# A two-layer decoder trunk on one core: the first transfers cut smaller and spread over both queues, the first x tile's upper part made on VectorE, ten warm-up products for fifteen

## Chip, core and metric

The kernel runs on one core of a Trainium2 chip. The metric is the time of one execution on the device in microseconds (us). The kernel before takes 419.99 us, the median of three runs from 419.8 to 420.08.

## What is computed

Two layers over x, 256 tokens of 1024 numbers in float32. Each layer normalises its input, projects it, mixes along the tokens, gates with SiLU and projects back. Layer 0, with whose first projection the kernel starts, is this:

```python
def rms_norm(x, g):
    xf = x.astype(jnp.float32)
    y = xf * lax.rsqrt(jnp.mean(xf * xf, axis=-1, keepdims=True) + EPS)
    return (y * g.astype(jnp.float32)).astype(x.dtype)

def pool_layer(x, norm_g, w_in, w_pool, pool_scale, w_out):
    h = rms_norm(x, norm_g)
    u, z = jnp.split(h @ w_in, 2, axis=-1)          # 1024 -> 2048 + 2048
    y = pool_mixer(u, w_pool, pool_scale) * jax.nn.silu(z)   # moving sums of 2, 4, 8, 16 tokens
    return x + y @ w_out                            # 2048 -> 1024
```

Layer 1 has the same frame with w_in 1024 -> 4 x 2048 (q, k, v, z) and causal attention in 16 heads of 128 as its mixer; with 256 tokens there is one block, and no block choice takes part.

## The kernel before

The order of the work is written out by hand: one program for each engine, tied by semaphores. SyncE (SP) and ScalarE (ACT) each issue transfers on a queue of their own; both queues are served by the same 16 DMA engines.

Every product of two float32 matrices is made as three products in fp32r: each operand is split into an upper part (rounded to fp32r, names ending in _hi) and a lower part (what is left, _lo), and hi x hi, hi x lo and lo x hi are added up. ScalarE makes the upper parts by copying (`w_hi`, line 413 for the first pieces; `hT_hi`, line 410, which also multiplies by the norm's gain), VectorE the lower parts by subtracting (`w_lo`, line 866; `hT_lo`, line 876).

The weights come in granules of 1 MB (four 128x512 blocks) into a ring of four buffers, `raw`. The first two granules belong to the first 512 columns of w_in0 and are loaded block by block, eight transfers of 256 KB on SP's queue (line 245), so that work can start on the first block. Meanwhile ScalarE's queue brings the norm's gains (16 KB, line 375) and x transposed, `xT` (part of the buffer `wide`; eight tiles of 128x256), as four transfers of 256 KB, two tiles in each (line 377).

The useful work starts in `early_granule`: eight stages, one for each x tile. In a stage TensorE multiplies one weight block by one x tile: four products hi x hi, four with `w_lo`, four with `hT_lo` (line 656). For stage i ScalarE makes `hT_hi` of tile i, then `w_hi` of block i; VectorE then makes `w_lo` of block i and `hT_lo` of tile i. TensorE waits for `h0_hi` and `piece_hi` ahead of a stage, for `piece_split` ahead of its second four products and for `h0_split` ahead of its third.

Until the data are there, TensorE runs 15 warm-up products of zeros (line 697), float32, 128x128, each of which is two passes in the trace. ScalarE's first instruction is a dummy exponential (line 379) that has the function table loaded early; in its program it stands behind the transfers that ScalarE issues.

Of the kernel before, what the change touches and what calls it, by code (L numbers as in the profile page):

```python
# [9 lines left out]
ALU = mybir.AluOpType  # L10
ACT = mybir.ActivationFunctionType
# [14 lines left out]
KD = D_MODEL // P  # L26
KI = D_INNER // P
COLS = 512
GK = 4
GROUPS = D_INNER // COLS  # L30
HPG = COLS // HEAD_DIM
RING = 4
EDGE = max(POOL_WINDOWS)
PADDED = EDGE + SEQ
WARM_UP = 15
MASKED = -1e30
NO_MAX = -3.4e38

# [15 lines left out]
def constant_tables():  # L54

    edge = np.stack([w / np.minimum(np.arange(EDGE) + 1, w) for w in POOL_WINDOWS]).astype(np.float32)
    edge = np.ascontiguousarray(np.broadcast_to(edge.reshape(1, -1), (P, GROUPS * EDGE)))
    inv = np.float32(ROPE_THETA) ** (-np.arange(0, HEAD_DIM, 2, dtype=np.float32) / np.float32(HEAD_DIM))
# [30 lines left out]
def bass_hybrid_trunk(nc, x, w_in0, w_pool0, w_out0, w_in1, w_out1, xT_in, gains_in, qk_gains, table, edge_table,  # L89
                      out):  # L90
    with ExitStack() as ctx:
        def sb(name, shape, dt=F32):
            return ctx.enter_context(nc.sbuf_tensor(name, shape, dt))

        def sem(name):
            return ctx.enter_context(nc.semaphore(name))


        raw = sb("raw", [P, RING, GK * COLS])
        w_hi = sb("w_hi", [P, RING, GK * COLS], F32R)  # L100
        w_lo = sb("w_lo", [P, RING, GK * COLS], F32R)
        xs = sb("xs", [P, TT, D_MODEL])
        hT_hi = sb("hT_hi", [P, KD, SEQ], F32R)
# [4 lines left out]
        uT = sb("uT", [P, HPG, PADDED])  # L108
        edges = sb("edges", [P, GROUPS, EDGE])
        rstd_b = sb("rstd_b", [P, SEQ])  # L110
# [10 lines left out]
        gains = sb("gains", [P, 2 * KD + KI])  # L121
# [28 lines left out]
        xT = wide[:, :, :].rearrange("p t n -> p (t n)")[:, 2 * D_MODEL:].rearrange("p (k s) -> p k s", k=KD)  # L150
# [19 lines left out]
        zeros_made = sem("zeros_made")  # L170
        raw_landed = [sem(f"raw_landed{i}") for i in range(RING)]
        ident_made, gains_landed = sem("ident_made"), sem("gains_landed")
        edges_landed, table_landed = sem("edges_landed"), sem("table_landed")
        diag_made, rstd_spread, rstd_b_made = sem("diag_made"), sem("rstd_spread"), sem("rstd_b_made")
        pooled_made = sem("pooled_made")
        x_landed, xT_landed = sem("x_landed"), [sem(f"xT_landed{b}") for b in range(KD // 2)]
        piece_landed = [[sem(f"piece_landed{n}{k}") for k in range(GK - 1)] for n in range(2)]
        piece_hi, piece_split = sem("piece_hi"), sem("piece_split")
        h0_hi, h0_split = sem("h0_hi"), sem("h0_split")
        half_hi = [sem("half_hi0"), sem("half_hi1")]  # L180
        half_split = sem("half_split")
        hi_made = sem("hi_made")
# [42 lines left out]
        w_in0_v = w_in0.rearrange("(k p) n -> p k n", p=P)  # L225
# [6 lines left out]
        def _(sp):  # L232
            def load(slot, src, n=None):
                if n is not None:
                    sp.wait_ge(w_split, n - RING + 1)
                sp.dma_start(raw[:, slot, :].rearrange("p (k n) -> p k n", k=GK), src).then_inc(raw_landed[slot], 16)
# [3 lines left out]
                load(j, src, n)  # L240


            for i in range(2 * GK):
                n, k = i // GK, i % GK
                sp.dma_start(raw[:, n, k * COLS:(k + 1) * COLS],
                             w_in0_v[:, i, 0:COLS]).then_inc((*piece_landed[n], raw_landed[n])[k], 16)
# [42 lines left out]
            for i in range(8 * GROUPS + 8):  # L289
# [8 lines left out]
                if i < 8 * GROUPS:  # L298
                    g, j = divmod(i, 8)
                    src = w_in1_v[:, (j % 2) * GK:(j % 2 + 1) * GK, bass.ds((j // 2) * D_INNER + g * COLS, COLS)]  # L300
                    load(j % RING, src, N_L1 + 8 * g + j)
                else:
# [70 lines left out]
        @block.scalar  # L373
        def _(act):
            act.dma_start(gains[:, :], gains_in).then_inc(gains_landed, 16)
            for b in range(KD // 2):
                act.dma_start(xT[:, 2 * b:2 * b + 2, :], xT_in[:, 2 * b:2 * b + 2, :]).then_inc(xT_landed[b], 16)
            act.wait_ge(pool_chain, 2)
            act.activation(row_sum[:, 0, 0:1], minus_half[:, 0:1], ACT.Exp)

# [24 lines left out]
            act.wait_ge(gains_landed, 16)  # L405
            for i in range(KD):
                n, k = i // GK, i % GK
                if i % 2 == 0:
                    act.wait_ge(xT_landed[i // 2], 16)
                act.activation(hT_hi[:, i, :], xT[:, i, :], ACT.Copy, scale=gains[:, i:i + 1]).then_inc(h0_hi, 1)  # L410
                act.wait_ge((*piece_landed[n], raw_landed[n])[k], 16)
                piece = slice(k * COLS, (k + 1) * COLS)
                act.activation(w_hi[:, n, piece], raw[:, n, piece], ACT.Copy).then_inc(piece_hi, 1)
            act.wait_ge(raw_landed[2], 16)
            act.activation(w_hi[:, 2, 2 * COLS:], raw[:, 2, 2 * COLS:], ACT.Copy).then_inc(half_hi[1], 1)
            for b in range(KD // 2):
                act.activation(sqT[:, 2 * b * SEQ:2 * (b + 1) * SEQ],
                               xT[:, 2 * b:2 * b + 2, :].rearrange("p k s -> p (k s)"),
                               ACT.Square).then_inc(sqT_made, 1)
# [188 lines left out]
        def _(pe):  # L608
# [32 lines left out]
            def u_tile(f):  # L641
                return acc[0][f // 2][:, (f % 2) * SEQ:(f % 2 + 1) * SEQ]

            def early_granule(n):

                for k, i, f in [(k, i, f) for k in range(GK) for i in range(3) for f in range(HPG)]:
                    if f == 0 and i == 0:
                        pe.wait_ge(h0_hi, GK * n + k + 1)
                        pe.wait_ge(piece_hi, GK * n + k + 1)
                    if f == 0 and i == 1:  # L650
                        pe.wait_ge(*((piece_split, (GK - 1) * n + k + 1) if k < GK - 1 else (w_split, n + 1)))
                    if f == 0 and i == 2:
                        pe.wait_ge(h0_split, GK * n + k + 1)
                    src, w = (hT_lo if i == 2 else hT_hi), (w_lo if i == 1 else w_hi)
                    c = k * COLS + f * P
                    ins = pe.matmul(u_tile(f), w[:, n, c:c + P], src[:, GK * n + k, :],  # L656
                                    start=(n, i, k, f % 2) == (0, 0, 0, 0), stop=(n, i, k) == (1, 2, GK - 1),
                                    skip_group_check=True)
                    if n == 1 and i == 2 and k == GK - 1 and f == 1:
                        ins.then_inc(tile0_ready, 1)  # L660
                ins.then_inc(w_used, 1)
# [33 lines left out]
            pe.wait_ge(zeros_made, 1)  # L695
            for _ in range(WARM_UP):
                pe.matmul(acc[1][1][:, 0:P], zeros, zeros, start=True, stop=True)  # L697

            early_granule(0)
            early_granule(1)  # L700

            def sum_tokens():
# [138 lines left out]
        def _(dve):  # L841
# [22 lines left out]
            def part_lo(n, a, b, made):  # L864
                part = slice(a * COLS, b * COLS)
                return dve.tensor_tensor(w_lo[:, n, part], raw[:, n, part], w_hi[:, n, part].bitcast(F32),
                                         ALU.subtract).then_inc(made, 1)

            def piece_lo(n, k):
                dve.wait_ge(piece_hi, GK * n + k + 1)  # L870
                part_lo(n, k, k + 1, piece_split if k < GK - 1 else w_split)

            for i in range(KD):
                piece_lo(i // GK, i % GK)
                dve.wait_ge(h0_hi, i + 1)
                dve.scalar_tensor_tensor(hT_lo[:, i, :], xT[:, i, :], gains[:, i:i + 1],
                                         hT_hi[:, i, :].bitcast(F32), ALU.mult, ALU.subtract).then_inc(h0_split, 1)
            dve.wait_ge(half_hi[0], 1)
# [11 lines left out]
            ins.then_inc(sqT_summed, 1)  # L890
            dve.memset(uT[:, :, 0:EDGE], 0.0)

            def u_out(g):
                for t in range(TT):
                    product_ready(dve, t, 2 * g, 4 * g + 1)
                    if t == 0:
                        dve.wait_ge(*((pooled_made, g) if g else (rstd_b_made, 1)))
                    dve.tensor_tensor(uT[:, 2 * t:2 * t + 2, EDGE:], acc[0][t][:, :].rearrange("p (f s) -> p f s", f=2),
                                      rstd_b[:, :].unsqueeze(1).to_broadcast([P, 2, SEQ]), ALU.mult).then_inc(u_made, 1)
# [58 lines left out]
            for g in range(GROUPS):  # L958
                n = N_POOL + 3 + g
# [152 lines left out]
            for j in range(6):  # L1112
# [6 lines left out]
                n = N_OUT1 + 3 + j  # L1119
# [39 lines left out]
```

## Time and profile before

| what | value |
|---|---|
| median of 3 runs | 419.99 us |
| the profiled execution | 419.89 us |
| its span, first to last instruction | 417.9 us |
| TensorE busy | 413.7 us, 99% of the span |
| VectorE, ScalarE, GpSimd busy | 292.2, 236.9, 32.0 us |
| TensorE's warm-up, line 697 | 1.04 to 7.57 us |

The span leaves out some 2 us around the program. All times within it count from its first instruction. A matmul's row in the trace overlaps with the next one's, since products are pipelined; the distance from start to start is what one costs.

### The profile page before, as it was taken

To read this page: it belongs to the slowest core of one execution; us is meant where nothing else is said; L and a number is where in the kernel's file an instruction comes from. 1 tells how busy PE (TensorE), PEld (TensorE's weight loads), DVE (VectorE), ACT (ScalarE), POOL (GpSimd) and SP (SyncE) were. 2 spreads that over 40 slices of the span, in tenths; PEclk is the share of its full clock that TensorE was granted. 3 is DMA by queue.
4 is the path that set the end of the run, shared out by engine and by line. 5 is a ranking of instruction groups with operands and counts; after the bars stand their busy time and mean duration, and the time that the engine had idled before them with its cause. 6 is when DMAs were issued, how large, how long until landed. Compare 5 with 4: busy or idle time off the path is not lost.

```text
span 417.9 us, 5551 instructions
## 1 busy us (share of the span) xinstructions
PE 413.7 (99%) x2126; PEld 354.6 (85%) x2126; DVE 292.2 (70%) x373; ACT 236.9 (57%) x430; POOL 32.0 (8%) x45
## 2 busy tenths in 40 slices
PE   9999999999999999999999999999999999999996
PEld 9989898988888888888888888888888888888885
DVE  3879987779885554428943799637996479966522
ACT  5845453525464353477837796377863978636310
POOL 0166000000000000111001010010000110000000
PEclk9999999999999999999999999999999999999999
DMA  7996769464554756337876627878478856767002
GB/s 268 385 351 217 262 199 341 152 209 169 210 177 132 207 190 201 102 100 252 300 233 221 192 103 262 254 228 273 129 263 262 249 206 183 226 245 252 0 2 100
DMA packets 45945, 86.78 MB, mean 208 GB/s; under 512 B 2528, under 2 KB 8288, under 8 KB 45920
## 3 DMA queue, kind: packets, MB, share of 16 engines
q1 hardware_dynamic: 45200, 85.37, 61.7%
q10 hardware_dynamic: 720, 1.07, 0.8%
q8 instruction: 17, 0.28, 0.3%
q14 instruction: 8, 0.07, 0.0%
HBM read 79.61 MB, written 6.82 MB: 207 GB/s over the span
## 4 chain that ended last, share of the span: by engine, by line
PE 99%; DVE 0%; issue 0%
PE acc L633 26%; PE acc L635 26%; PE acc L634 26%; PE acc L678 3%; PE acc L677 3%; PE acc L656 3%; PE acc L675 3%; PE aux L772 2%; PE acc L697 2%; PE aux L688 1%; PE aux L779 1%; PE aux L790 1%; PE aux L791 1%; PE aux L789 1%; PE aux L771 1%; DVE ysb L1129 0%
## 5 line engine op out<-in xcount | busy, mean ns | idle before, releaser
L848 DVE TENSOR_TENSOR w_lo<-raw,w_hi 128x2048 fp32r<-128x2048 f32 x65 | 147.9, 2285 | 45.2 <-ACT w_hi L384 45.2
L384 ACT ACTIVATE w_hi<-raw 128x2048 fp32r<-128x2048 f32 x64 | 122.0, 1914 | 43.9 <-PE acc L635 31.0
L633 PE MATMUL acc<-w_hi,hT_hi 128*128 128x512 f32 x320 | 127.0, 397 | 0.0
L635 PE MATMUL acc<-w_hi,hT_lo 128*128 128x512 f32 x320 | 124.8, 390 | 0.0
L634 PE MATMUL acc<-w_lo,hT_hi 128*128 128x512 f32 x320 | 124.6, 389 | 0.0
L635 PEld LDWEIGHTS acc<-w_hi,hT_lo 128*128 128x128 f32 x320 | 60.1, 188 | 12.8
L634 PEld LDWEIGHTS acc<-w_lo,hT_hi 128*128 128x128 f32 x320 | 60.2, 188 | 11.9
L633 PEld LDWEIGHTS acc<-w_hi,hT_hi 128*128 128x128 f32 x320 | 60.1, 188 | 11.8
L633 PE MATMUL acc<-w_hi,aT_hi 128*128 128x512 f32 x160 | 63.6, 397 | 0.0
L635 PE MATMUL acc<-w_hi,aT_lo 128*128 128x512 f32 x160 | 62.4, 390 | 0.0
L634 PE MATMUL acc<-w_lo,aT_hi 128*128 128x512 f32 x160 | 62.3, 389 | 0.0
L635 PEld LDWEIGHTS acc<-w_hi,aT_lo 128*128 128x128 f32 x160 | 30.0, 188 | 6.4
L634 PEld LDWEIGHTS acc<-w_lo,aT_hi 128*128 128x128 f32 x160 | 30.1, 188 | 5.9
L633 PEld LDWEIGHTS acc<-w_hi,aT_hi 128*128 128x128 f32 x160 | 30.1, 188 | 5.8
L1004 DVE CUSTOM_DVE_ANT_0 aux<-aux,mask 128x128 f32<-128x128 f32 x16 | 4.7, 296 | 37.1 <-PE aux L772 37.1
L677 PE MATMUL acc<-hT_hi,w_hi 128*128 128x256 f32 x96 | 27.2, 283 | 0.0
L678 PE MATMUL acc<-hT_lo,w_hi 128*128 128x256 f32 x96 | 27.2, 283 | 0.0
L675 PE MATMUL acc<-hT_hi,w_lo 128*128 128x256 f32 x96 | 27.2, 283 | 0.0
L483 ACT ACTIVATE probs<-aux,exp_bias,q_rstd 128x128 f32<-128x128 f32 x16 | 7.2, 451 | 26.7 <-DVE exp_bias L1008 26.6
L675 PEld LDWEIGHTS acc<-hT_hi,w_lo 128*128 128x128 f32 x96 | 18.4, 192 | 0.1
L677 PEld LDWEIGHTS acc<-hT_hi,w_hi 128*128 128x128 f32 x96 | 18.4, 192 | 0.1
L678 PEld LDWEIGHTS acc<-hT_lo,w_hi 128*128 128x128 f32 x96 | 18.4, 192 | 0.0
(126 smaller groups left out, 452.4 us busy)
## 6 DMA issues: line engine op xcount, KB each, us to landing
raw<-in_w_in_dram SPq DMA_DIRECT2D x46, 1024.0 KB, 7.0
raw<-in_w_out_dram SPq DMA_DIRECT2D x16, 1024.0 KB, 5.4
raw<-in_w_pool_dram SPq DMA_DIRECT2D x4, 1024.0 KB, 5.6
between<-wide SPq DMA_DIRECT2D x8, 512.0 KB, 3.9
raw<-in_w_in_dram SPq DMA_DIRECT2D x8, 256.0 KB, 8.0
wide<-between SPq DMA_DIRECT2D x16, 128.0 KB, 2.8
qkT<-between SPq DMA_DIRECT2D x16, 128.0 KB, 3.0
between<-uT SPq DMA_DIRECT2D x3, 512.0 KB, 10.1
```

The costliest lines, as they stand in the source:

```text
L384: act.activation(w_hi[:, slot, :], raw[:, slot, :], ACT.Copy).then_inc(hi_made, 1)
L483: act.activation(probs[:, 0:P], aux[h % 2][:, 0:P], ACT.Exp, bias=exp_bias[:, h, 0:1], scale=q_rstd[:, g % 2, 0, h:h + 1], accum_out=row_s ...
L633: pe.matmul(a, shi, whi, start=first and k == 0, stop=False)
L634: pe.matmul(a, shi, wlo, start=False, stop=False)
L635: ins = pe.matmul(a, slo, whi, start=False, stop=last and k == GK - 1)
L656: ins = pe.matmul(u_tile(f), w[:, n, c:c + P], src[:, GK * n + k, :], start=(n, i, k, f % 2) == (0, 0, 0, 0), stop=(n, i, k) == (1, 2, GK ...
L675: pe.matmul(u_tile(f), wlo, shi, start=j == 0 and k == 0 and f % 2 == 0, stop=False, skip_group_check=True)
L677: pe.matmul(u_tile(f), whi, shi, start=False, stop=False, skip_group_check=True)
L678: ins = pe.matmul(u_tile(f), whi, slo, start=False, stop=end, skip_group_check=True)
L697: pe.matmul(acc[1][1][:, 0:P], zeros, zeros, start=True, stop=True)
L772: pe.matmul(s[:, P:3 * P], qT[:, h, P:SEQ], kT[:, :, h], start=True, stop=True).then_inc(scores_ready, 1)
L848: dve.tensor_tensor(w_lo[:, slot, :], raw[:, slot, :], w_hi[:, slot, :].bitcast(F32), ALU.subtract).then_inc(w_split, 1)
```

## The change

Five edits, all at the start of the program.

- The first weight block (256 KB) is cut in two halves of 256 columns. SP issues the first half as before at the head of its queue, ScalarE issues the second half.
- ScalarE issues x in five pieces instead of four: tile 0, tile 1, then the pairs 2 and 3, 4 and 5, 6 and 7. The half weight block goes out right behind tile 0.
- VectorE makes `hT_hi` of tile 0 with its own semaphore `first_h0_hi`; ScalarE's loop starts with the first weight block and goes on with tile 1.
- TensorE waits for `first_h0_hi` in the first stage, and the counts of `h0_hi` are one lower in the others.
- Ten warm-up products instead of fifteen.

```diff
+X_PIECES = [(0, 1), (1, 2), (2, 4), (4, 6), (6, 8)]
-WARM_UP = 15
+WARM_UP = 10
...
-            for i in range(2 * GK):
+            sp.dma_start(raw[:, 0, 0:COLS // 2], w_in0_v[:, 0, 0:COLS // 2]).then_inc(piece_landed[0][0], 16)
+            for i in range(1, 2 * GK):
                 n, k = i // GK, i % GK
                 sp.dma_start(raw[:, n, k * COLS:(k + 1) * COLS],
                              w_in0_v[:, i, 0:COLS]).then_inc((*piece_landed[n], raw_landed[n])[k], 16)
...
-            for b in range(KD // 2):
-                act.dma_start(xT[:, 2 * b:2 * b + 2, :], xT_in[:, 2 * b:2 * b + 2, :]).then_inc(xT_landed[b], 16)
+            for b, (k0, k1) in enumerate(X_PIECES):
+                act.dma_start(xT[:, k0:k1, :], xT_in[:, k0:k1, :]).then_inc(xT_landed[b], 16)
+                if b == 0:
+                    act.dma_start(raw[:, 0, COLS // 2:COLS], w_in0_v[:, 0, COLS // 2:COLS]).then_inc(piece_landed[0][0], 16)
...
-                if i % 2 == 0:
-                    act.wait_ge(xT_landed[i // 2], 16)
-                act.activation(hT_hi[:, i, :], xT[:, i, :], ACT.Copy, scale=gains[:, i:i + 1]).then_inc(h0_hi, 1)
-                act.wait_ge((*piece_landed[n], raw_landed[n])[k], 16)
+                if i > 0:
+                    for b, (k0, _) in enumerate(X_PIECES):
+                        if k0 == i:
+                            act.wait_ge(xT_landed[b], 16)
+                    act.activation(hT_hi[:, i, :], xT[:, i, :], ACT.Copy, scale=gains[:, i:i + 1]).then_inc(h0_hi, 1)
+                act.wait_ge((*piece_landed[n], raw_landed[n])[k], 16 if i > 0 else 32)
...
-                        pe.wait_ge(h0_hi, GK * n + k + 1)
+                        pe.wait_ge(*((h0_hi, GK * n + k) if n or k else (first_h0_hi, 1)))
                         pe.wait_ge(piece_hi, GK * n + k + 1)
...
+            dve.wait_ge(gains_landed, 16)
+            dve.wait_ge(xT_landed[0], 16)
+            dve.tensor_scalar(hT_hi[:, 0, :], xT[:, 0, :], gains[:, 0:1], 1.0, ALU.mult, ALU.mult).then_inc(first_h0_hi, 1)
             for i in range(KD):
                 piece_lo(i // GK, i % GK)
-                dve.wait_ge(h0_hi, i + 1)
+                dve.wait_ge(*((h0_hi, i) if i else (first_h0_hi, 1)))
```

ScalarE's program from its start, before the change; `gains`, `wide` (x transposed) and `raw` (weights) are filled by its and SP's transfers, and what it waits for stands in brackets:

```order
L375 DMA gains<-in_gains_dram 128x32
L377 DMA wide<-in_xT_dram 128x512 x4
L379 ACT_TABLE_LOAD
L379 ACTIVATE row_sum<-minus_half 128x1 [waits pool_chain]
L410 ACTIVATE hT_hi<-wide,gains 128x256 [waits xT_landed0,gains_landed]
L413 ACTIVATE w_hi<-raw 128x512 [waits piece_landed00]
L410 ACTIVATE hT_hi<-wide,gains 128x256
L413 ACTIVATE w_hi<-raw 128x512 [waits piece_landed01]
```

The same stretch after the change:

```order
L377 DMA gains<-in_gains_dram 128x32
L379 DMA wide<-in_xT_dram 128x256
L381 DMA raw<-in_w_in_dram 128x256
L379 DMA wide<-in_xT_dram 128x256
L379 DMA wide<-in_xT_dram 128x512 x3
L383 ACT_TABLE_LOAD
L383 ACTIVATE row_sum<-minus_half 128x1 [waits pool_chain]
L419 ACTIVATE w_hi<-raw 128x512 [waits piece_landed00,gains_landed]
L416 ACTIVATE hT_hi<-wide,gains 128x256 [waits xT_landed1]
L419 ACTIVATE w_hi<-raw 128x512 [waits piece_landed01]
L416 ACTIVATE hT_hi<-wide,gains 128x256 [waits xT_landed2]
```

Seven transfers instead of five stand ahead of the table load, and the first `w_hi` is ScalarE's first piece of real work. VectorE's program after the change, from its first instruction:

```order
L850 MEMSET k_s 128x128
L882 TENSOR_SCALAR hT_hi<-wide,gains 128x256
L873 TENSOR_TENSOR w_lo<-raw,w_hi 128x512
L886 SCALAR_TENSOR_TENSOR hT_lo<-wide,gains,hT_hi 128x256
L873 TENSOR_TENSOR w_lo<-raw,w_hi 128x512
```

Its second row is new; before, the first `w_lo` (line 866) stood right behind the memset, and all that follows is as it was.

## Rows read from the trace of the kernel before

**Rows 1.** The page: span, TensorE's busy time, granted clock in 40 slices.
```profile
span 417.9 us, 5551 instructions
PE 413.7 (99%) x2126; PEld 354.6 (85%) x2126; DVE 292.2 (70%) x373; ACT 236.9 (57%) x430; POOL 32.0 (8%) x45
...
PEclk9999999999999999999999999999999999999999
```

**Rows 2.** TensorE's waits in the whole span: us in total, times, longest.
```profile
PE acc L697 <- DVE k_s L843: 1.0, 1, 1.0
```

**Rows 3.** The chain that ended last: start us, us, what (three pieces).
```profile
1.04 6.53 PE acc L697 x30
7.56 11.52 PE acc L656 x96
...
109.10 0.87 PE aux L688 x8
```

**Rows 4.** The head in order of time: start us, us, engine, line, what.
```profile
1.16 2.01 ACTq L377 DMA_DIRECT2D wide<-in_xT_dram  x4
...
3.19 1.28 ACT L379 ACT_TABLE_LOAD   x1 [3.19 <-issue]
4.49 0.20 ACT L379 ACTIVATE row_sum<-minus_half 128x1 f32<-128x1 f32 x1
...
5.95 0.51 ACT L410 ACTIVATE hT_hi<-wide,gains 128x256 fp32r<-128x256 f32 x1 [1.26 <-DMA wide<-in_xT_dram]
6.37 0.61 ACT L413 ACTIVATE w_hi<-raw 128x512 fp32r<-128x512 f32 x1
...
7.01 0.69 DVE L866 TENSOR_TENSOR w_lo<-raw,w_hi 128x512 fp32r<-128x512 f32 x1 [6.03 <-ACT w_hi L413]
...
7.62 0.48 DVE L876 SCALAR_TENSOR_TENSOR hT_lo<-wide,gains,hT_hi 128x256 fp32r<-128x256 f32 x1
...
8.84 0.64 PE L656 MATMUL acc<-hT_hi,w_hi 128*128 128x256 f32 x4
...
10.28 0.64 PE L656 MATMUL acc<-hT_hi,w_hi 128*128 128x256 f32 x4
```

**Rows 5.** DMA issues at 0.7, 1.2, 1.8, 2.3 us: KB each, us to landing.
```profile
raw<-in_w_in_dram SPq DMA_DIRECT2D x1, 256.0 KB, 3.4
gains<-in_gains_dram ACTq DMA_DIRECT2D x1, 16.0 KB, 3.5
...
wide<-in_xT_dram ACTq DMA_DIRECT2D x1, 256.0 KB, 4.7
raw<-in_w_in_dram SPq DMA_DIRECT2D x1, 256.0 KB, 4.5
...
raw<-in_w_in_dram SPq DMA_DIRECT2D x1, 256.0 KB, 6.0
wide<-in_xT_dram ACTq DMA_DIRECT2D x1, 256.0 KB, 6.6
...
raw<-in_w_in_dram SPq DMA_DIRECT2D x1, 256.0 KB, 7.5
wide<-in_xT_dram ACTq DMA_DIRECT2D x1, 256.0 KB, 7.7
```

**Rows 6.** When the last two pairs of these were issued: start us, us.
```profile
1.64 0.45 ACTq L377 DMA_DIRECT2D wide<-in_xT_dram  x1
...
2.12 0.45 ACTq L377 DMA_DIRECT2D wide<-in_xT_dram  x1
```

**Rows 7.** DMA queues from 2.0 to 3.0 us: packets, MB, share of 16 engines.
```profile
q1 hardware_dynamic: 118, 0.22, 81.4%
q10 hardware_dynamic: 105, 0.02, 13.6%
```

**Rows 8.** Stretches at the end: us, busy of PE, PEld, DVE, ACT, POOL; clock; DMA.
```profile
414.00:415.00 1.00, 0.75 (x4) 0.29 (x2) 0.21 (x1) 0.00 (x0) 0.00 (x0) 1.00 0.32 121
...
416.80:417.90 1.10, 0.00 (x0) 0.00 (x0) 0.00 (x0) 0.00 (x0) 0.00 (x0) 0.50 0.22 80
```

More of the change, by code:

```diff
@@ L175, in bass_hybrid_trunk @@
         pooled_made = sem("pooled_made")
-        x_landed, xT_landed = sem("x_landed"), [sem(f"xT_landed{b}") for b in range(KD // 2)]
+        x_landed, xT_landed = sem("x_landed"), [sem(f"xT_landed{b}") for b in range(len(X_PIECES))]
         piece_landed = [[sem(f"piece_landed{n}{k}") for k in range(GK - 1)] for n in range(2)]
         piece_hi, piece_split = sem("piece_hi"), sem("piece_split")
-        h0_hi, h0_split = sem("h0_hi"), sem("h0_split")
+        first_h0_hi, h0_hi, h0_split = sem("first_h0_hi"), sem("h0_hi"), sem("h0_split")
         half_hi = [sem("half_hi0"), sem("half_hi1")]
@@ L415, in _ @@
             act.activation(w_hi[:, 2, 2 * COLS:], raw[:, 2, 2 * COLS:], ACT.Copy).then_inc(half_hi[1], 1)
+            act.wait_ge(xT_landed[0], 16)
             for b in range(KD // 2):
```

## The prediction

> **What bounds the kernel now.** I read the page first [rows 1]: TensorE is busy 413.7 of the 417.9 us of the span. Then TensorE's list of waits [rows 2], which has one entry in the whole run, 1.0 us ahead of the very first warm-up product. So from 1.04 us to the end TensorE always has something to do, and what stands in its way is its own stream. Time can be won in one place only: the 30 warm-up passes (15 products, two passes each) take 6.53 us [rows 3] and compute nothing. The first useful product starts where they end, at about 7.3 us. Whatever the change does to the start of the third stage of useful products (one stage = the 12 products of one x tile, 1.44 us from 8.84 to 10.28 [rows 4]) goes through to the end one for one, since no later wait exists that could swallow it.
>
> Next I read the head in order of time [rows 4]. ScalarE makes the first x tile's upper part at 5.95 and the first weight piece's at 6.37, done at 6.98. The warm-up ends some 0.3 us after that, so before the change the data are nearly in step with the warm-up: the cut of five warm-up products is worth 0.3 us unless the data come earlier too.
>
> Last, the clock. The 30 warm-up passes are 0.218 us apart; eight passes of the same shape at 109 us take 0.87 us, 0.109 each [rows 3]. The warm-up runs at the lower of the two levels (1.2 GHz), the useful products from 7.3 us at the upper (2.4 GHz), though the page's row of the granted clock shows nine tenths or more in every slice [rows 1]. TensorE had worked without a break since 1.04 when the pace rose. At the other end the last products are issued before 415 us, and by 416.80 the granted clock is 0.50 [rows 8]: some 2 us of rest were enough to lose it there.
>
> **The change part by part.** I call the place where stage 3 starts S3; before, it is 10.28 [rows 4].
>
> *Ten warm-up products.* Twenty passes at 6.53/30 = 0.218 us end at 1.04 + 4.36 = 5.4 us.
>
> *The x tile's upper part on VectorE.* One instruction of 128x256 in place of ScalarE's 0.51 us [rows 4]. VectorE's other operation on that form lasts 0.48 us (the row at 7.62), and VectorE has nothing to do before 7.01, so this is free as long as the 128 KB x piece lands before about 5.9. It is the second issue of its queue, and the 256 KB piece there now landed at 1.16 + 4.7 = 5.9 [rows 5], half of it must be earlier. Behind it nothing waits but the lower parts, which need the weight piece anyway.
>
> *ScalarE's issues.* It now issues seven transfers before its table load in place of five. Four take 2.01 us [rows 4], so the load moves from 3.19 to 4.2; with 1.28 and 0.20 us ScalarE is free at 5.7. That is the floor: weight piece made by 5.7 + 0.61 = 6.3 at the earliest.
>
> *The landings.* This is the large term. The first weight piece (256 KB, head of SP's queue) now lands at 0.72 + 3.4 = 4.1 [rows 5]. Its second half moves behind the gains and the first x piece on ScalarE's queue. How the two queues share the DMA engines can be read between 2 and 3 us [rows 7]: 118 packets of q1 (SP) and 105 of q10 (ScalarE), although q1 moved 0.22 MB and q10 0.02. They take turns by packets, whatever their size. The changed pieces of ScalarE's queue have rows of 1 KB against SP's 2 KB, so SP gets two bytes for each of theirs. Counting what both queues must have moved before a piece is there: now 272 KB (gains, weight piece 0) at 4.2; 784 KB at 5.7 to 5.9; 1296 KB at 7.6 to 8.2; 1808 KB at 9.6 to 9.8 [rows 5, 6]. After, by turns: weight half 0b needs 16 + 128 + 128 on ScalarE's queue and 128 + 256 + 256 on SP's, 912 KB: 5.8 + 0.25 x 2.1 = 6.3. The second x piece needs 1296 KB: 7.9. The x pair 2 and 3 needs 1808 KB: 9.7. That is the upper end. Lower end, equal bytes: 544 KB at 5.05, 800 KB at 5.9, 1312 KB at 8.2. I take the turns, which the row shows.
>
> The Trainium skill ("DMA: Bandwidth & Descriptors", section "Rules for kernel authors") says that spreading transfers over queues of several engines brings no bandwidth, since all run on the same 16 engines, and only saves issue time. By it the move of the half to the other queue neither helps nor harms and the lower end would hold; the packets of [rows 7] say that it harms a queue with shorter rows.
>
> *The start, T.* Half 0b at 6.3, 0.09 us to react (as 5.86 to 5.95), 0.61 us on ScalarE: useful products start at T = 7.05 in place of 7.32, **-0.3 us**. Between 5.4 and 7.05 TensorE now rests 1.6 us, where before it had no rest.
>
> *Stages 1 and 2 with the upper clock.* The lower part of the weights comes 0.72 us after the upper one (6.98 to 7.70 [rows 4]) and is wanted 0.48 us after the start, so stage 1 takes about 1.65 us. x piece 2 at 7.9 plus 0.1, 0.51 and 0.6 us less their overlap of 0.09: stage 2 starts at 9.05 (8.84 before). x pair 2 and 3 at 9.7: in the same way the weights of stage 3 are ready at 10.8, S3 = 10.85, **+0.55 us**. Behind that all pieces are early enough (ScalarE needs 1.0 us per stage of 1.44).
>
> *The clock.* No row shows useful products at the lower level; a stage would take 2 x 1.44 = 2.88 us there, half of each such microsecond is lost. Lower end: the rest is not noticed and the clock rises at 7.2 as now, cost 0.1 us. Upper end: the rise is earned anew, 6.1 us of unbroken work after T (7.17 less 1.04), at 13.15. The row nearest to a rest of 1.6 us is the end of the run, where 2 us lose the clock; that speaks against the lower end. What was done before the rest may still count in part, so I take the middle, a rise at about 10.1. Then stage 1 runs 7.05 to 9.93, stage 2 starts then (its data are there at 9.05), does 0.09 us' worth by 10.1 and ends at 11.45. S3 = 11.45, **+1.2 us**; the late landing (10.85) is hidden behind it.
>
> The Trainium skill ("TensorE: Matmul & The Clock Gate", Part 1) says that the lower level is the default that recent activity lifts, and that the moment of the rise differs from run to run of one kernel. The end of the run agrees with the first. By the second, the executions of the changed kernel would scatter between the times of rivals A and C below, where those of before lie within 0.28 us; one profile cannot show it.
>
> **Sum.** The profiled execution took 419.89 us (span 417.9 and 2.0 around it), 0.1 under the median of 419.99. 419.89 + 1.17 = 421.1.
>
> **Rivals.**
> - *Forecast: late clock, half way.* Rise between 9 and 11.5: S3 between 10.9 and 12.15, 420.5 to 421.8.
> - *A: the clock comes up in time, the landings decide.* For it: the rise at 7.17 came only just as useful work began, and the rest falls beside low demand. S3 = 10.85: 420.4 (419.9 to 420.8). No change that can be told.
> - *B: faster.* One mechanism: the queues share by bytes. Half 0b lands at 5.05, ScalarE's table load is the floor, T = 6.3, the rest shrinks to 0.9 us and the clock rises as before or sooner; stage 1 ends 7.95, stage 2 9.4, the x pair lands at 8.2 and is worked up by 9.3, so S3 = 9.45: -0.83, 419.1. It decides from the point where half 0b is there before 5.7. Against it stand [rows 7]. It is also the case in which the change does what it says.
> - *C: the clock is earned wholly anew.* Rise at 13.15: stages 1 and 2 end at 12.81, 0.17 us are lost in stage 3, +2.7: 422.6.
>
> **Chances.** Forecast 0.42, A 0.28, B 0.16, C 0.14. About 0.2% (0.84 us) is what can be told from no change here. Slower by more: 0.36 of the forecast's, all of C: 0.50. Faster by more: 0.10 of B, whose time lies at that bound, and 0.04 out of A for landings earlier than any row suggests: 0.14. Within: 0.36. The range leaves out the better half of B and the worse half of C: 419.2 to 422.4; the forecast's own is 420.5 to 421.8.
>
> **What would show it.** The landing of the weight half on ScalarE's queue: by 6.3 for me, by 5.1 for B. TensorE's waits: a gap of 1.6 us after the warm-up (0.9 for B). The pace of the first useful products: 0.24 us apart for the forecast and C, 0.12 for A and B, and where it doubles. The start of the third stage: 11.45, 10.85, 9.45 or 12.8. If the first useful products start before 6.4 at 0.12 us apart, my reading of the queues is wrong; if they start near 7 but at full pace, that of the clock is.

## The result, and the profile after

The changed kernel takes 421.66 us, the median of six runs from 421.25 to 423.16, against 419.92 (419.8 to 420.08) before: a ratio of 1.0046, with a 95% interval of 1.0035 to 1.0057. It is slower by 1.7 us, and its runs lie seven times as far apart as those of before. The profiled execution is the slowest of the six, 423.16 us with a span of 421.2, and the only one with a trace. That the landings are as late in the other five, and that their clock behaves in the same way, is not shown by it.

TensorE's list of waits, of the whole span, answers to [rows 2] (us in total, times, longest):

```profile
PE acc L663 <- ACT w_hi L419: 2.2, 1, 2.2
PE acc L704 <- DVE k_s L850: 1.0, 1, 1.0
```

One wait is new: 2.2 us ahead of the first useful product, for the upper part of the first weight block. The chain that ended last says where that comes from; its head answers to [rows 3] (start us, us, what):

```profile
1.64 5.33 DMA raw<-in_w_in_dram
...
7.06 0.64 ACT w_hi L419
...
7.83 14.44 PE acc L663 x96
```

Before, the chain began with TensorE's own warm-up. Now a transfer heads it: the second half of the first weight block, issued by ScalarE at 1.64, lands at 6.97. The eight stages (96 products) take 14.44 us where they took 11.52. TensorE's head in order of time shows why (start us, us, engine, line, what, count, idle time before):

```profile
7.83 1.19 PE L663 MATMUL acc<-hT_hi,w_hi 128*128 128x256 f32 x4 [2.16 <-ACT w_hi L419]
...
10.53 1.05 PE L663 MATMUL acc<-hT_hi,w_hi 128*128 128x256 f32 x4
...
13.09 1.03 PE L663 MATMUL acc<-hT_hi,w_hi 128*128 128x256 f32 x4
...
14.43 0.64 PE L663 MATMUL acc<-hT_lo,w_hi 128*128 128x256 f32 x4
14.91 0.64 PE L663 MATMUL acc<-hT_hi,w_hi 128*128 128x256 f32 x4
```

Four products span 1.05 us up to the third stage, and 0.64 from 14 us on: the first two stages and part of the third run at the lower clock. This is read from the pace. The granted clock does not show it in this trace (1.00 from 7.90 to 13.90 us; the row has us, busy us of PE, PEld, DVE, ACT, POOL with instruction counts, granted clock, DMA share, GB/s):

```profile
7.90:13.90 6.00, 6.00 (x28) 6.00 (x29) 5.15 (x11) 5.25 (x12) 0.00 (x0) 1.00 1.05 396
```

The same pace stands beside a granted clock of 0.50 in the kernel before with ten warm-up products, below, and that ties it to the lower level. From 10.53 to 13.09 a stage takes 2.56 us in place of 1.44. The third stage starts at 13.09, 2.8 us later than before [rows 4], another 0.4 us goes in the part of it that still runs slowly, and the span is 3.3 us longer: to 0.1 us, nothing behind that point swallows any of it or adds to it.

The landings, of the same issues as [rows 5] (KB, us from issue to landing; the issues are those of 0.72, 1.15, 1.64, 2.12 and 2.6 us):

```profile
raw<-in_w_in_dram SPq DMA_DIRECT2D x1, 128.0 KB, 2.2
gains<-in_gains_dram ACTq DMA_DIRECT2D x1, 16.0 KB, 2.4
...
wide<-in_xT_dram ACTq DMA_DIRECT2D x1, 128.0 KB, 3.7
...
raw<-in_w_in_dram ACTq DMA_DIRECT2D x1, 128.0 KB, 5.3
...
wide<-in_xT_dram ACTq DMA_DIRECT2D x1, 128.0 KB, 5.9
...
wide<-in_xT_dram ACTq DMA_DIRECT2D x1, 256.0 KB, 7.1
```

The pieces at the heads of the queues are earlier than before (the first x tile is there at 4.9, the first half block at 2.9), those behind them later: the whole first block was there at 4.1 and is now complete at 6.97, the x pair 2 and 3 went from 8.2 to 9.7.

### The profile page after: what moved, and what is told of

Read it like the earlier page. It is cut to its first block, busy times and chain, and to the rows that moved or that the text cites. A ratio compares the mean times of both kernels' runs of the same rounds, so it can differ in the third digit from the quotient of the medians.

```text
span 421.2 us, 5534 instructions
## 1 busy us (share of the span) xinstructions
PE 414.7 (98%) x2116; PEld 355.4 (84%) x2116; DVE 293.3 (70%) x374; ACT 236.5 (56%) x429; POOL 32.7 (8%) x45
## 4 chain that ended last, share of the span: by engine, by line
PE 97%; DMA 1%; ACTq 0%; DVE 0%; ACT 0%; issue 0%
PE acc L640 26%; PE acc L642 26%; PE acc L641 26%; PE acc L663 3%; PE acc L685 3%; PE acc L684 3%; PE acc L682 3%; PE aux L779 2%; PE aux L695 1%; DMA raw<-in_w_in_dram 1%; PE aux L786 1%; PE aux L797 1%; PE aux L798 1%; PE aux L796 1%; PE aux L778 1%; DVE ysb L1139 0%
## 5 line engine op out<-in xcount | busy, mean ns | idle before, releaser
L640 PEld LDWEIGHTS acc<-w_hi,hT_hi 128*128 128x128 f32 x320 | 60.1, 188 | 11.8
```

Of the source, the lines that this page charges most:

```text
L640: pe.matmul(a, shi, whi, start=first and k == 0, stop=False)
```

## The experiments

The two causes to be told apart are the late landing of ScalarE's pieces and TensorE's rest ahead of the useful work, which costs the clock. Behind each median stand its lowest and highest time. The experiments ran in three jobs, each on another chip and each beside runs of the kernel before (medians 419.94, 420.01 and 420.06); the kernels of different jobs are best compared by what they lie above or below those.

**The changed kernel without the rest.**

```diff
-WARM_UP = 10
+WARM_UP = 15
```

> The changed kernel with 15 warm-up products, so that TensorE works from 1.04 to 7.6 us and rests at most 0.3 us before the useful products. Theory (the rest before the first useful product costs the clock, the late half block costs the rest): useful products start at 7.8 as in the changed kernel, at 0.12 us apart within 0.3 us of it, the third stage starts at 10.7 to 11.0, 420.4 to 420.8 us, and the runs lie within 0.4 us. Rival (the landings alone make it slower): no change, 421.4 to 421.9 and the same scatter of 1.9 us.

Measured: 420.84 us (420.53 to 421.12, 11 runs), ratio to before 1.0018 (1.0010 to 1.0027). The useful products start where they did in the changed kernel, but at full pace:

```profile
7.84 0.71 PE L663 MATMUL acc<-hT_hi,w_hi 128*128 128x256 f32 x4 [0.75 <-ACT w_hi L419]
...
9.52 0.64 PE L663 MATMUL acc<-hT_hi,w_hi 128*128 128x256 f32 x4
...
10.96 0.40 PE L663 MATMUL acc<-hT_hi,w_hi 128*128 128x256 f32 x2
```

The third stage starts at 10.96. What is left, 0.9 us over before (1.0 when this kernel ran again, below), is the landings' share. The changed kernel lay 1.7 us over before, so five warm-up products give back 0.7 to 0.8 us; the two did not run in one job. The scatter is 0.6 us here and 1.3 in the repeat, against 1.9. The rest was 0.75 us in this run, more than expected: warm-up passes that run at the upper clock end earlier.

**The rest alone, in the kernel before.**

```diff
-WARM_UP = 15
+WARM_UP = 10
```

> The kernel before with ten warm-up products and nothing else: TensorE rests from 5.4 to 7.0 us, no landing is touched. Theory (rest costs the clock): useful products start at 7.0, 0.3 us earlier than before, but 0.21 us apart until some moment between 9.5 and 13.2; 420.8 to 422.3 us, with a scatter of more than 0.5 us. Rival (landings alone): 0.3 us faster than before, 419.6, no scatter.

Measured: 421.13 us, and two groups: four runs from 419.92 to 420.07, eight from 421.01 to 422.47. The rival is out, and the theory has the amount right but not the form: it is not a late rise in every run. In the profiled one (421.85) the clock was lost after the useful work had begun. The x pair also came later in this run (6.4 us for 5.9), so TensorE rested longer than the 1.6 us expected. Stretches of that run (start:end, us; busy us of PE, PEld, DVE, ACT, POOL with instruction counts; granted clock; DMA share; GB/s):

```profile
5.80:7.50 1.70, 0.00 (x0) 0.00 (x0) 0.02 (x1) 1.08 (x3) 0.00 (x0) 1.00 0.96 328
7.70:8.30 0.60, 0.60 (x5) 0.47 (x5) 0.60 (x2) 0.60 (x3) 0.00 (x0) 1.00 1.06 372
8.45:11.75 3.30, 3.30 (x17) 3.30 (x17) 3.11 (x7) 2.90 (x7) 0.00 (x0) 0.50 1.05 401
11.85:14.00 2.15, 2.15 (x20) 2.15 (x19) 2.15 (x5) 2.15 (x6) 0.00 (x0) 1.00 1.05 391
```

TensorE rested for 2.2 us, began useful work at 7.6 with the clock at the upper level, and then ran at half of it from 8.4 to 11.8, though it worked without a break. 17 products in 3.3 us stand there against 20 in 2.15 behind it (one that crosses an edge is counted), and four span 1.05 us, as in the changed kernel:

```profile
9.99 1.05 PE L656 MATMUL acc<-hT_hi,w_hi 128*128 128x256 f32 x4
```

The mean granted clock of every run is on record. This run has 0.996, since 3.4 us at half clock are 0.4% of the span. Three more of the eight slower runs have 0.996 too, the other four have 0.999 or 1.00; the four of the first group have 1.00. A clock that rises late does not show in that number (the changed kernel's trace has 0.999), so what slowed the last four stays open. The gain that fewer warm-up products were to bring does not show even in the first group: 419.92 to 420.07 is the time of before.

**The first block whole again.**

```diff
-            sp.dma_start(raw[:, 0, 0:COLS // 2], w_in0_v[:, 0, 0:COLS // 2]).then_inc(piece_landed[0][0], 16)
-            for i in range(1, 2 * GK):
+            for i in range(2 * GK):
...
-                if b == 0:
-                    act.dma_start(raw[:, 0, COLS // 2:COLS], w_in0_v[:, 0, COLS // 2:COLS]).then_inc(piece_landed[0][0], 16)
```

> The changed kernel with the first weight block whole at the head of SP's queue, so that ScalarE's queue brings x only, in its five pieces; ten warm-up products. Theory: the block lands at 4.1 to 4.3, ScalarE's table load (six issues ahead of it) becomes the floor, useful products start at 6.2 to 6.6; the rest is about 1 us, the clock still comes late in most runs: 419.8 to 421.8 us, 0.5 to 1 us under the changed kernel. Rival (it is the clock alone, the half block costs nothing): within 0.3 us of the changed kernel.

Measured: 421.67 us (420.86 to 421.92, 5 runs), the time of the changed kernel. By the number the rival won; the trace shows that neither theory nor rival was right. The block lands at 4.04 and useful products start at 6.29, as the theory had it, and they start at full pace in the profiled run (421.71). The loss moved to x (TensorE's rows; then the landing of the pair 2 and 3, issued at 2.12):

```profile
6.29 0.71 PE L660 MATMUL acc<-hT_hi,w_hi 128*128 128x256 f32 x4 [1.37 <-ACT w_hi L416]
...
8.36 0.71 PE L660 MATMUL acc<-hT_hi,w_hi 128*128 128x256 f32 x4 [0.22 <-ACT w_hi L416]
...
11.81 0.71 PE L660 MATMUL acc<-hT_hi,w_hi 128*128 128x256 f32 x4 [1.61 <-ACT w_hi L416]
```

```profile
wide<-in_xT_dram ACTq DMA_DIRECT2D x1, 256.0 KB, 8.5
```

The pair lands at 10.6, the third stage waits for it until 11.81. TensorE waits 3.2 us in all, in three places. So an earlier start alone buys nothing while the third stage is bound by the x pair. Why the pair is so late is shown in part only. Counted in turns as in the prediction, 1552 KB stand ahead of it, which is about 8.8 us on its line (an estimate), against 8.2 before: that is what the cut of x into 1 KB rows can account for. A landing is made up of 16 shares, whose moments are in the trace: 13 of them were there by 8.96, the last three at 9.41, 10.01 and 10.62. Those three are not explained.

**Are the turns counted in packets?** The bytes stay, SP's blocks 1 and 2 get rows of 1 KB:

```diff
+                if i < 3:
+                    for c in (0, COLS // 2):
+                        sp.dma_start(raw[:, n, k * COLS + c:k * COLS + c + COLS // 2],
+                                     w_in0_v[:, i, c:c + COLS // 2]).then_inc(piece_landed[n][k], 16)
+                    continue
```

> The changed kernel, in which SP's weight blocks 1 and 2 are each cut into two transfers with rows of 1 KB instead of 2 KB: the bytes and their order stay, SP has twice the packets in them. Theory (the two queues take turns by packets): ScalarE's half block needs as many turns as before, in which SP now moves 256 KB less, so it lands earlier than the 6.97 us of the changed kernel, by about a microsecond (5.8 to 6.2), and the second x tile likewise (6.6 to 7.2 for 8.03); useful products start at 6.6 to 7.0. SP's block 2 lands later (about 8). Rival (the queues share by bytes, the pieces are late for another reason): landings within 0.2 us of the changed kernel's. The time itself scatters by the clock, 420.5 to 422.

Measured: 420.29 us (419.7 to 421.04, 10 runs), ratio 1.0003 (0.9989 to 1.0016): 0.3 us over before, where the changed kernel lay 1.7 over. The same two issues of ScalarE's queue, at 1.64 and 2.12:

```profile
raw<-in_w_in_dram ACTq DMA_DIRECT2D x1, 128.0 KB, 3.3
...
wide<-in_xT_dram ACTq DMA_DIRECT2D x1, 128.0 KB, 5.0
```

The half block lands 2.0 us earlier (4.95 for 6.97), the second x tile 0.9 us (7.1 for 8.0). How the queues share can be read from 4 to 7 us (packets, MB, share of 16 engines; q1 is SP's queue, q10 ScalarE's). The changed kernel:

```profile
q1 hardware_dynamic: 329, 0.60, 59.3%
q10 hardware_dynamic: 318, 0.31, 33.4%
```

With the short rows on SP:

```profile
q10 hardware_dynamic: 305, 0.39, 46.0%
q1 hardware_dynamic: 324, 0.32, 39.4%
```

The packets are nearly equal in both, the bytes are not. So the theory holds: the queues share by packets, and SP's packets of twice the size made the half block late. Not all of the 2.0 us is due to that. On the chip of this run the half block of the changed transfers landed at 6.6 (in the next experiment), which leaves 1.7. And the middle one of its 16 shares moved by 1.2 us, from 5.7 to 4.5, about as expected. The rest is in the last three shares: in the changed kernel they came at 6.29, 6.46 and 6.97, behind the others at 5.84; here the last of all was there at 4.95.

The Trainium skill ("DMA: Bandwidth & Descriptors", section "Queues, rings and completion order") says that an engine takes turns between queues by whole packets, typically of some 9 to 17 descriptors. That the turns go by packets agrees with these counts; what takes a turn here is a packet of the profile, a single row, and not a group: in the kernel before 35 rows of SP's queue and 26 of ScalarE's stand side by side between 2.0 and 2.3 us, when each of the 16 shares of a transfer has eight rows and none has landed before 2.98.

**What VectorE's tile is worth.** In the changed kernel with 15 warm-up products, ScalarE makes the first tile again:

```diff
-                if i > 0:
+                if True:
...
-            dve.tensor_scalar(hT_hi[:, 0, :], xT[:, 0, :], gains[:, 0:1], 1.0, ALU.mult, ALU.mult).then_inc(first_h0_hi, 1)
```

> The changed kernel with 15 warm-up products, in which ScalarE makes the first x tile's upper part again. Theory (ScalarE waits for the half block anyway, from about 6.0 to 6.97): the tile's part, 0.5 us, fits into that wait, and the time is that of the changed kernel with 15 warm-up products, 420.84 within 0.2 us. Rival (VectorE's help is worth its 0.5 us): 421.3.

Measured: 421.31 us (420.43 to 422.32), 0.5 above the kernel that it is to be compared with, which ran in another job on another chip. That speaks for the rival; but in the trace the tile lies inside the wait and the weight part begins right behind the landing (6.64 for 6.62). What is later there is the x pair 2 and 3, at 10.3 for 9.6, on transfers that are the same in both. So both were run again side by side.

> The changed kernel with 15 warm-up products once more, beside the next one on the same chip. 420.6 to 421.1 us, as before, if chip and moment matter little; if the landings scatter by chip, up to 421.4.

> The same with ScalarE making the first x tile's upper part, on the same chip as the one before. Theory (the part fits into ScalarE's wait for the half block): within 0.2 us of it. Rival (VectorE's help is worth its 0.5 us there): 0.4 to 0.5 us above it.

Measured: 421.09 (420.27 to 421.57) and 421.06 us (420.8 to 423.7). ScalarE in the second:

```profile
5.91 0.20 ACT L383 ACTIVATE row_sum<-minus_half 128x1 f32<-128x1 f32 x1
6.02 0.49 ACT L416 ACTIVATE hT_hi<-wide,gains 128x256 fp32r<-128x256 f32 x1
6.60 0.63 ACT L419 ACTIVATE w_hi<-raw 128x512 fp32r<-128x512 f32 x1
```

The tile fits in: VectorE's help is worth nothing where the half block is late. The 0.5 us of the first pair is a difference between jobs, and nothing here rests on one of that size.

**VectorE's tile where nothing is late.** The transfers of before, VectorE's tile 0, 12 warm-up products:

```diff
+X_PIECES = [(0, 2), (2, 4), (4, 6), (6, 8)]
-WARM_UP = 15
+WARM_UP = 12
...
+            dve.tensor_scalar(hT_hi[:, 0, :], xT[:, 0, :], gains[:, 0:1], 1.0, ALU.mult, ALU.mult).then_inc(first_h0_hi, 1)
```

> The transfers as before the change; of the change only VectorE's upper part of the first x tile stays, with 12 warm-up products that end at 6.3. Theory: the x pair lands at 5.9 as before, VectorE's part is ready at 6.3 and ScalarE's weight piece at 5.4, so useful products start at 6.35 without a rest, at 0.21 us apart until about 7.2, and the third stage starts at 9.6: 419.3 us (419.0 to 419.7), faster than before. Rival (TensorE's start is set elsewhere, or the clock comes later with fewer warm-up products): 419.9 or more.

Measured: 419.51 us (419.19 to 420.12, 11 runs), ratio 0.9987 (0.9979 to 0.9996): faster than before, if by little. Useful products start at 6.38, the third stage at 9.80, where ScalarE has to make tile and block after the pair's landing.

> The kernel before with 12 warm-up products, which end at 6.3, and nothing else: beside the kernel with VectorE's tile and 12 warm-up products (419.51) it tells what the tile alone is worth. Theory: useful products start at 7.0 after a rest of 0.8 us; where the clock holds 419.6, where it comes late up to 421.5; median 419.7 to 420.6 with a scatter over 0.6 us. Rival (fewer warm-up products alone made that kernel faster): 419.5, no scatter.

Without the tile, 12 warm-up products give 420.06 us: eight runs from 419.87 to 420.18, four from 422.32 to 423.39. Those four have a mean granted clock of 0.996 or less, the eight have 1.00: they lost the clock. The eight gain nothing either: in the profiled one useful products start at 7.27, no more than 0.05 us earlier than before, and the first stage, which now starts by its data, takes 1.70 us (to 8.97) where it took 1.52. Fewer warm-up products are not the gain; they are a risk.

**The next bound.** VectorE makes tile 2 as well, so that ScalarE can turn to the third block as soon as that is there:

```diff
-                if i > 0:
+                if i not in (0, 2):
...
+                if i == 2:
+                    dve.wait_ge(xT_landed[1], 16)
+                    dve.tensor_scalar(hT_hi[:, 2, :], xT[:, 2, :], gains[:, 2:3], 1.0, ALU.mult, ALU.mult).then_inc(first_h0_hi, 1)
```

> The kernel with the transfers of before, 12 warm-up products and VectorE's upper part of x tile 0, in which VectorE also makes the upper part of tile 2, so that ScalarE can make the third weight block while the x pair is still on its way. Theory (the third stage started at 9.80 because ScalarE makes both after the pair landed at 8.6): the third stage starts when the second ends, at about 9.5 us, 0.3 us earlier: 419.2 us. Rival (the block itself lands too late, or the clock sets the pace): 419.4 to 419.6, no gain.

Measured: 419.30 us, ten runs from 419.09 to 419.49 and two at 421.86 and 422.15; with those two the ratio is 0.9986 (0.9967 to 1.0006), which does not yet tell it from before. In the profiled run the third stage starts at 9.72, when the second ends, as the theory had it. The middle of the ten lies 0.8 us under before; the kernel with tile 0 alone lay 0.4 under it in its own job. The two have a mean granted clock of 0.996: VectorE's tiles do not take the risk away. Then the same with more warm-up products:

> The kernel in which VectorE makes the upper parts of x tiles 0 and 2, with the transfers of before, and 14 warm-up products instead of 12 (28 passes, the last starts at 6.8 us at the lower clock, useful products could start at 6.6). Theory (two of twelve runs with 12 products fell to 422 because TensorE rested 1 us and lost the clock): fewer or none of the runs above 421, median 419.1 to 419.4, under the kernel before by 0.5 to 0.8 us. Rival (the high runs have another cause): as many high runs as with 12.

> The same with 17 warm-up products, whose last pass starts at 8.1 us if the clock stays low so long and at about 6.3 if it rises at 4.5. Theory: TensorE hardly rests in any run, so no run lies above 420.5; where the clock rises late the useful work starts up to 0.7 us later than it could: 419.2 to 419.9, median 419.4. Rival (high runs have another cause): some runs at 421 to 423 remain.

Measured: with 14, 419.39 us (419.10 to 420.40, 11 runs), ratio 0.9983 (0.9975 to 0.9992); with 17, 419.69 us (419.20 to 420.55), ratio 0.9988 (0.9977 to 0.9999). No run at 421 or above in either, and no mean granted clock under 0.999. That is in line with the theory, but 0 of 22 against 2 of 12 does not prove it. With 14, TensorE's head reads:

```profile
6.94 0.72 PE L660 MATMUL acc<-hT_hi,w_hi 128*128 128x256 f32 x4
...
9.89 0.64 PE L660 MATMUL acc<-hT_hi,w_hi 128*128 128x256 f32 x4
```

Its third stage starts 0.4 us before that of before, without a wait. This version beats both kernels, by 0.7 us against before in its own job (420.06).

## Why the prediction was right, and where it was not

*That it is slower:* right, and by the two causes forecast, the late half block and the rest that costs the clock. The sum had +0.55 us for the landings and 0.6 more for the clock; measured are 0.9 to 1.0 (the changed kernel with 15 warm-up products against before) and 0.7 to 0.8 (what it lies above that with ten). That the median also fell into the forecast's own range (420.5 to 421.8) is in part luck, since its form of the clock's loss is in no trace (below).

*The landings.* The turns by packets were right, and shown by the run with short rows on SP. The step from there to the time of the half block was mis-sized: 912 KB at 6.3, called the upper end, came at 6.97 (6.5 to 7.0 in the four other traces with these transfers). I took the bytes that both queues had to move ahead of a landing and a straight line between two landings. The queues were not slower than that line: by 7 us they had moved 1.47 MB, against 1.45 before. But a landing comes with the last of its 16 shares. Thirteen shares of the half block were there by 5.84, ahead of the forecast; the last three came at 6.29, 6.46 and 6.97, as those of SP's block beside it did (the last at 6.78). The line had no term for that. Why these shares are late is not shown. The second x tile (7.9 forecast, 8.03) and the pair (9.7, 9.66) came out, but in the other traces with the same transfers the pair lands at 9.6 to 10.3.

*The start.* 7.05 forecast, 7.83 measured, 0.67 of it from the half block and the rest from the step between ScalarE's end and the first product (0.14 us, 7.69 to 7.83, where the sum had 0.05); with it the rest was 2.2 us and not 1.6. ScalarE's floor was also off, harmlessly: seven issues held the table load back to 4.80 in the profiled run, not 4.2.

*VectorE's tile for free:* right, it takes 0.35 us, but it also buys nothing there (421.09 with it, 421.06 without).

*The clock.* The forecast's place was between a rise that does not notice the rest and one that is earned anew in full. The profiled run is the second (rival C): the pace rises at 14 us, 6.1 after useful work began. All six times lie above the forecast's 421.1: four in its own range, two beyond it, at 422.33 and 423.16. What the record has of the six speaks for a third form: 421.64, 421.69 and 422.33, with the median between the first two, have mean granted clocks of 0.994 and 0.996, like the runs that had the upper level and lost it again; 421.25, 421.30 and 423.16 have 0.999 or 1.00. So no run shows the rise half way at 10.1 us, on which the sum stands, and the two runs at the median most likely paid in another way; none of the three was traced. A stage at the lower clock was mis-sized: 2.56 us, not 2.88, since the distance of these products does not double (0.213 for 0.12 us). The Trainium skill's statement ("TensorE: Matmul & The Clock Gate", Part 1) that the moment of the rise differs between runs of one kernel, which the prediction could not show, agrees with the two traced runs of the changed kernel with 15 warm-up products: its 30 passes took 6.04 us in one and 5.21 in the other. The 6.1 us that the prediction took from one trace are therefore no fixed figure.

*What the prediction left out:* a stage whose start is set by its weight block takes 1.69 us (6.29 to 7.98 with the block whole), as counted for the first stage, but the third stage was given 1.44, which leaves 0.25 us out of rival A's price; and with ten warm-up products the rest can cost a clock that had already risen.

*Rival B* (the queues share by bytes) is out. *Rival A*, the landings alone, is the kernel with 15 warm-up products, 420.84 and 421.09 for 420.4.

One thing stays open: why some runs lose the clock and others of the same kernel don't. The traced length of the rest does not sort them: 0.75 us with four of twelve runs lost (the kernel before with 12 warm-up products), 1.24 us with none of eleven (the repeat with 15). One trace shows where it was lost, none what decides it.

## What to carry to other kernels

A transfer cut in pieces and spread over two queues was not served by its bytes here: look how many packets stand ahead of each piece on both queues, and keep the rows of the urgent queue at least as long as the other's. Trim a warm-up only to where the data really arrive in the slowest run; twelve products in place of fifteen in the kernel before brought eight of twelve runs nothing and cost the other four 2.3 to 3.4 us. And before the start is made earlier, find what the second and third stage wait for.

## What had not been expected of the hardware

TensorE's clock can fall after work has resumed: in the kernel before with ten warm-up products it was at the upper level when useful work began at 7.6 us and at the lower from 8.4 to 11.8. The distance of the 128x256 fp32r products grows from 0.12 to 0.213 us there, a factor of 1.78. Cutting two transfers of another queue into rows of half the length brought a 128 KB transfer forward from 6.97 to 4.95 us (6.62 on the same chip). The last three of its 16 shares held that transfer's landing back by 1.1 us in the changed kernel. And the kernel before is not free of lost clocks either: among its 29 to 35 runs in each job, one lies at 422.7 to 423.4 us with a mean granted clock of 0.996, though its warm-up leaves no rest in the traced run.
